# Two-block fp32 transformer on one NeuronCore: the low halves of 16 weight tiles move from GpSimd to the vector engine

## The reference, cut to what matters

```
h    = rmsnorm(x);  proj = h @ w_in[l]          # six parts of width 512
sb   = stick_breaking_attention(sb_q, sb_k, sb_v)   # 8 heads of 64
df   = differential_attention(rope(df_q), rope(df_k), df_v)   # 4 heads of 128
x    = x + concat(sb, norm(df)) @ w_o[l]
h    = rmsnorm(x)
x    = x + square(relu(h @ w_ff1[l])) @ w_ff2[l]
```

## Time and profile before

| what | value |
|---|---|
| median of 3 runs | 1548.05 us (1547.95 to 1548.31) |
| the profiled execution | 1547.81 us, its span 1546.1 us |
| PE busy | 1530.1 us, 99% of the span |
| DVE busy | 1060.1 us, 69% |
| ACT busy | 821.3 us, 53% |
| GpSimd busy | 180.1 us, 12% |
| mean granted TensorE clock | 1.000 |

### The profile page before, as it was taken

How to read it: one execution, slowest core, us unless ns; L and a number is a source line. 1 busy time by engine, 2 the same in 40 slices (tenths; PEclk the granted TensorE clock), 3 DMA queues, 4 the chain that set the end, 5 groups by cost and what they waited for, 6 DMA issues and landing times.

```text
span 1546.1 us, 23494 instructions
## 1 busy us (share of the span) xinstructions
PE 1530.1 (99%) x8781; PEld 1293.7 (84%) x8781; DVE 1060.1 (69%) x1778; ACT 821.3 (53%) x1403; POOL 180.1 (12%) x146
## 2 busy tenths in 40 slices
PE   8999999999999999999999999999999999999998
PEld 7777888877888778898989888888788898989987
DVE  6886557566776876875858555775785875848653
ACT  5556533545655864645445335664874645545332
POOL 3001222032000313010100011000223010000001
PEclk9999999999999999999999999999999999999999
DMA  5211223322221113332332323212112233232331
GB/s 184 70 56 55 82 93 98 109 96 82 82 82 56 55 55 96 109 106 86 103 98 99 109 82 104 88 55 82 55 56 82 83 109 109 83 109 82 109 110 55
DMA packets 127300, 135.83 MB, mean 88 GB/s; under 512 B 2458, under 2 KB 120804, under 8 KB 127204
## 3 DMA queue, kind: packets, MB, share of 16 engines
q1 hardware_dynamic: 126048, 133.18, 26.8%
q0 software_dynamic: 288, 1.05, 0.2%
q10 hardware_dynamic: 868, 0.31, 0.1%
HBM read 132.43 MB, written 2.10 MB: 87 GB/s over the span
## 4 chain that ended last, share of the span: by engine, by line
PE 89%; DVE 4%; ACT 3%; issue 3%; POOL 1%; DMA 1%; DVEq 0%; SPq 0%; ACTq 0%; POOLq 0%
PE U L2002 19%; PE U L2004 19%; PE U L2003 19%; PE Z L2353 3%; PE Z L2354 3%; PE Z L2352 3%; PE U L2047 2%; PE U L2049 2%; PE U L2048 2%; PE U L2354 1%; PE U L2352 1%; PE U L2353 1%; PE Z L2242 1%; PE O L2294 1%; PE Z L2227 1%
## 5 line engine op out<-in xcount | busy, mean ns | idle before, releaser
L2002 PE MATMUL U<-MH,WL 128*128 128x512 f32 x848 | 336.7, 397 | 1.9 <-DVE tb L1648 1.7
L2004 PE MATMUL U<-MH,WH 128*128 128x512 f32 x848 | 330.6, 390 | 0.0
L2003 PE MATMUL U<-ML,WH 128*128 128x512 f32 x848 | 330.3, 389 | 0.0
L1165 DVE TENSOR_TENSOR WL<-raw,WH 128x1024 fp32r<-128x1024 f32 x181 | 234.7, 1296 | 81.3 <-ACT WH L654 72.3
L2002 PE MATMUL U<-XH,WL 128*128 128x512 f32 (+1 forms) x600 | 238.6, 398 | 1.5 <-DVE WL L1492 1.1
L2004 PE MATMUL U<-XH,WH 128*128 128x512 f32 (+1 forms) x600 | 232.5, 388 | 0.0
L2003 PE MATMUL U<-XL,WH 128*128 128x512 f32 (+1 forms) x600 | 232.0, 387 | 0.0
L654 ACT ACTIVATE WH<-raw 128x1024 fp32r<-128x1024 f32 x197 | 205.7, 1048 | 19.1 <-PE Z L2354 16.7
L2002 PEld LDWEIGHTS U<-MH,WL 128*128 128x128 f32 x848 | 159.2, 188 | 43.4 <-issue 8.5
L2004 PEld LDWEIGHTS U<-MH,WH 128*128 128x128 f32 x848 | 159.2, 188 | 34.0
L2003 PEld LDWEIGHTS U<-ML,WH 128*128 128x128 f32 x848 | 159.4, 188 | 31.8 <-issue 0.7
(11 more groups left out here) (306 smaller groups left out, 3060.7 us busy)
## 6 DMA issues: line engine op xcount, KB each, us to landing
raw<-in_w_ff SPq DMA_DIRECT2D x64, 1024.0 KB, 5.4
raw<-in_w_in SPq DMA_DIRECT2D x24, 1024.0 KB, 5.1
raw<-in_attn_w_in SPq DMA_DIRECT2D x9, 1024.0 KB, 5.3
raw<-in_pool_w_in SPq DMA_DIRECT2D x8, 1024.0 KB, 5.3
raw<-in_w_o SPq DMA_DIRECT2D x8, 1024.0 KB, 5.0
raw<-in_attn_w_out SPq DMA_DIRECT2D x4, 1024.0 KB, 5.2
raw<-in_pool_w_out SPq DMA_DIRECT2D x4, 1024.0 KB, 5.0
xin<-in_x SPq DMA_DIRECT2D x2, 1024.0 KB, 6.5
```

What stands on the lines that cost most here:

```text
L1165: v.tensor_tensor(w_slot(WL, t, shape), src, w_slot(WH, t, shape).bitcast(F32), ALU.subtract).then_inc(lo_done, 1)
L2002: mm(o, wl, xh, start=first, stop=False, **kw)
L2003: mm(o, wh, xl, start=False, stop=False, **kw)
L2004: return mm(o, wh, xh, start=False, stop=last, **kw)
```

## The change

The tuple of slots whose low halves GpSimd makes becomes empty in both layers. `low_here` is then true in slots 18 to 25, and DVE's `conv` runs there at the place shown above. `pool_tiles` is empty, so PE and SP wait on `lo_done` for all tiles. GpSimd's loop over `POOL_LOW[l]`, with its waits on the scans, has no turns. Its other work is as before.

```diff
-    POOL_LOW = {0: range(18, 26), 1: range(18, 26)}
+    POOL_LOW = {0: (), 1: ()}
```

## The result

The changed kernel takes **1565.46 us** (median of 4, 1564.57 to 1565.75) against 1548.0 (median of 4). The ratio is 1.0112, interval 1.0100 to 1.0123. The forecast was 1564.3, in a range from 1556 to 1568. The profiled execution has a span of 1563.6 us, 17.5 more than before.

The account below looks back on a forecast made before the run. PE, busy 99% of the span, was taken as the bound. Its lateness per layer was the largest single lateness less slack, not a sum: 2 x 8.26 = 16.5 us on 1547.8 gave 1564.3, range 1556 to 1568.

Parts of the forecast that it names:

- The bound: PE is busy 99% of the span; each new DVE instruction's place in the chain ACT, DVE, ACT, PE decides.
- Even slots, 2.08 us: In even slots DVE waits 0.94 us for ACT's high half and subtracts for 1.14, ahead of round 0's guard.
- The carried delay: DVE's lateness carries from pair to pair: first guards 2.08, 5.30, 7.38 and 8.88 us late.
- 20.8 to 21.0: Sign to look for: us from one pair's first guard to the next, where 17.7, 18.7 and 19.9 stood.
- What reaches PE: PE's lateness is the largest of DVE's lateness less slack: 2.1, 5.5, 7.4, then 8.26 us per layer.
- The eviction of turn 3: Turn 4 of pair 3 on PE needs turn 3 evicted by DVE; slack 0.50 us, so PE is 8.26 late.
- The chain of 5.88 us between pairs: From a pair's last subtraction to the next first guard: exponential, softplus, high half and subtraction, a fixed 5.88 us.
- The term put at nothing: SP's loads wait for DVE's low halves, about 2.6 us later at first; read over 15 us later, cost nothing.
- 1552: Rival 1: the delay does not carry, each pair starts afresh, 2.1 us lost per layer, 1552.0 us; chance 0.10.
- rival 3: GpSimd's subtraction holds up DVE; without it PE's four waits go, at most 1.1 us per layer, 1545.6; chance 0.02.

Follow-up runs that it names:

- the kernel with 8 columns: The kernel before, with GpSimd subtracting only 8 of 1024 columns of its tiles in slots 18 to 25, the rest not computed: 1548.41 against 1548.4 us.
- the doubled kernel: The change, with DVE's subtraction made twice in each of the even slots 18, 20, 22 and 24: 1577.42 us against 1548.33 for the kernel before.
- the change with the second order: The change, with ACT taking the exponential of round 1 ahead of the eviction of turn 1 in pairs 1 to 3: 1565.7 us against the change's 1565.46.

## Why the prediction was right

- **The bound.** The place in the chain decides, not DVE's idle time. The same eight tiles cost 0.7 us in odd slots and 8.9 in even ones.
- **Even slots, 2.08 us.** Measured by slot 18 alone at 2.25 per layer. That the wait for the high half matters shows in moving the high half ahead, which left 0.5 of the 17.5 us, and, with round 0 let ahead too, in moving the subtraction, which left 8.6.
- **The carried delay.** Forecast for the four first guards: 2.08, 5.30, 7.38, 8.88 us. Measured, less 0.76: 2.15, 5.42, 7.55, 9.00. From the end of a pair's last subtraction to the next guard it takes 5.94, 5.95 and 5.94 us, forecast 5.88. The stretches between guards are 20.9, 20.9 and 21.4; the "20.8 to 21.0" of my last section was a slip, as my own list gives 21.4 for the third.
- **What reaches PE.** Forecast 5.5 at slot 23, 7.4 at slot 25, 8.26 at the last turn; measured 5.8, 7.6 and 8.42. The eviction of turn 3 is the last releaser, as forecast, by 0.53.
- **A dependence I left out.** PE's scores of round 2 overwrite the bank that the subtraction of round 0 reads, and wait for it (1.65 us in pair 0). ACT's evictions, for which PE waits 0.9 us in the first two pairs, are not in my list either. The sum stood all the same: at turn 2 of pair 0, which waits for DVE's chain anyway, PE was 2.13 late, forecast 2.1.
- **A rule used outside its range.** The chain of 5.88 us between pairs holds when DVE is late. In the change DVE is always late from pair 1 on, so the sum stood; for a single tile in slot 24 it did not.
- **The term put at nothing.** The loads that now wait for DVE's low halves held nobody up: in the stage PE has no wait for a weight's low half or for SP.
- **Rivals.** The delay does carry, so 1552 is out. GpSimd held nobody up. The price I gave rival 3, at most 1.1 us per layer from PE's waits, was too small: taking away three of the four waits gave 1.34 per layer. The Trainium skill (SBUF — State Buffer, "Who interferes with whom") makes contention possible for a DVE instruction with two SBUF inputs; here no gain came from removing nearly all of GpSimd's work (1548.41 against 1548.4), and nearly all of DVE's instructions beside GpSimd's tiles have an input in PSUM; a scan, which has both in SBUF, lies beside one of them for 0.06 us in layer 0.
- **Left over.** 17.5 against 16.5 forecast. The two stages took 8.42 and 8.40 where I had 8.26 each; that is 0.3. The profiled execution also began its stage 0.76 late. That is not the change's: the stage begins 0.75 late as well in the kernel with 8 columns, which has GpSimd's tiles in place, and 0.34 to 0.75 late in all eleven kernels of the experiments. The execution of the kernel before that I compare with was an early one. The medians, too, differ by 17.5, and 0.6 of that lies outside the stages' cost. In the other series the kernel before took 1548.3 to 1548.45, not 1548.0, which is up to 0.45 of it; the rest stays open.

## What to carry to other kernels

In a loop over several in-order queues, price a moved instruction by what it waits for and by what stands behind it, not by its own length: here 1.14 us of work cost 2.1 where it waited for a half that another queue made late, and 0.1 (0.7 for eight) where that half was ready and the queue had idle time. Before moving work to another engine, look whether the producer can be moved ahead into one of its own waits; that gave back 17.0 of 17.5 us without touching the moved work. Delays add up along the chain, and what reaches the engine that bounds the kernel is the largest lateness less its slack. The slack can be used only once, so single costs measured alone (0.7 and 8.9) say little about the pair (17.5), and a gain measured in one kernel (2.7) may be nothing in the next.

## What the runs showed of the hardware

PE's granted clock fell below 1.00 after some of PE's waits in the stage, and was back at 1.00 after one or two stretches of 4 us. In the doubled kernel it fell after all four waits of 2.91 to 3.14 us (0.86 and 0.71 in two stretches of 4 us after the first, 0.57 in one stretch of 4 us, 1106 to 1110, after the one at 1106.34). Waits of about 2 us came out either way. In the doubled kernel the clock fell to 0.57 in 1174 to 1178 with a wait of 1.86 at 1174.18, and stayed at 1.00 with one of 1.87 at 575.47. In the change with the second order it fell after the waits of 2.01 and 2.00 at 569.97 and 1163.70, and not after those of 2.05 and 2.06 at 548.38 and 1142.10. So the length of the wait alone doesn't decide it. With the first of the two drops went 0.4 us (8.80 against 8.42 late at the last turn, with slot 25 begun at the same lateness). In the profiled execution of the change, whose longest wait of PE in the stages was 1.9 us, no stretch of 4 us there was below 1.00. The means over its four executions were 0.995 to 0.999, where those of the kernel before were 0.999 to 1.000 in the other series, so some of them may have lost a little there.

A wait of the transposes is larger than the wait that PE's matmul rows show: at turn 2 of pair 1 the matmul row has 0.23 us, the row of the weight load ahead of it 0.67, and 0.41 came back when the cause was taken away.
